# One core's mixture-of-experts tail: the last two experts' rows added on chip, the closing work dealt to three engines

## The chip, the cores and the metric

The kernel runs on one core of one Trainium2 chip. The metric is the time of one execution in device microseconds (us), the median of three runs. Beside it stands one execution recorded by the hardware profiler, from which every row below is taken. TensorE is called PE in the rows, VectorE DVE, ScalarE ACT, GpSimd POOL, SyncE SP.

## What is computed

One transformer layer for 256 prompt tokens and 64 sample tokens, 320 in all, with model width 1024, in float32. The change concerns only its last part: a mixture of 32 experts, of which each token takes two, and the closing layer norm.

```python
def hier_moe(h, p):                      # tok: 320 x 1024
    ...                                  # eid, w2: two experts of one group and their shares
    combine = jnp.einsum('nk,nke->ne', w2, jax.nn.one_hot(eid, N_EXPERTS, dtype=jnp.float32))
    y = jnp.zeros(tok.shape, jnp.float32)
    for e in range(N_EXPERTS):
        he = jax.nn.silu(tok @ p['w_exp_gate'][e]) * (tok @ p['w_exp_up'][e])
        y = y + combine[:, e:e + 1] * (he @ p['w_exp_down'][e]).astype(jnp.float32)
    ...
def trunk_layer(...):
    ...
    x = layer_norm(DEEPNORM_ALPHA * x + gate_f[:, None] * hier_moe(h, p), p['ln2_g'], p['ln2_b'])
```

## The kernel before

The program is written engine by engine, each engine's instructions in the order of the code; semaphores join them (`then_inc` counts up when an instruction is done, `wait_ge` holds an engine until a count is reached). After attention and routing, the kernel goes through the 32 experts one by one. Each expert has 64 slots, and each of its three weight matrices is 2 MB; SP loads them into a ring of nine buffers (`expert_chunk`), three experts deep, each load waiting until the buffer's former contents were used.

For one expert, in `step` on each engine: POOL gathers the token rows of the expert's slots from DRAM (`gather`, line 617), TensorE turns them (line 1448) and multiplies by gate and up matrices (`gate_up`, line 1458), ACT takes the silu (`silu`, line 959), DVE multiplies (`gated`, line 2022), TensorE turns the hidden rows (`turn_hidden`, line 1470), DVE copies them (`turned`, line 2026), TensorE multiplies by the down matrix (`down`, line 1481), and DVE scales the 64 result rows by the token's share and the condition's gate into a buffer `ystage` (`rows_out`, lines 2006 and 2012). POOL then scatters `ystage` into a DRAM table `expert_rows` (`scatter`, line 626). The table has four rows of 512 per token: two halves of width for each of its two experts. Which token sits in which slot is a one-hot table `onehot` (tokens by slots), written by DVE in `one_hots` and used by TensorE in `index` (line 1417). For tokens beyond an expert's 64 slots there is a loop over extra rounds (`n_over` of them), behind a branch on each engine; with these inputs it is not entered, as the trace has 32 scatters for 32 experts.

After expert 31 the end begins. POOL waits until every scatter has landed (`scattered0` to `scattered2`) and loads the table back, for the three token tiles in the order 0, 2, 1 (128, 64 and 128 tokens) into `comb[t]` (line 667), two rows of 1024 for a token side by side. `comb` lies in ring buffers 3 and 4, and the closing norm's vectors `ln2` in ring buffer 5, loaded by POOL once expert 29 is done with it (lines 647 and 648). TensorE adds in PSUM: for each tile a product of the identity with the scaled residual `x1` (line 1550), and products of the identity with each of the two rows in `comb[t]` (line 1556). DVE then handles the tiles one after another: statistics (lines 2116 and 2118), subtract the mean and multiply by the norm's weight (line 2122), the inverse deviation (lines 1579 to 1589, after ACT's square root at line 729), and multiply and add the bias (line 2125). ACT stores each tile (line 999), and the kernel ends when the last store has landed.

```python
            for t in LAST_ORDER:
                m = TR[t]
                pe.wait_ge(S[f"comb_in{t}"], 16)
                for c in range(2):
                    for k in range(2):
                        last = mm(fin_bank(t, c), ident[0:m, 0:m], comb[t][0:m, k * D + c * CB:k * D + c * CB + CB],
                                  start=False, stop=(k == 1))
                last.then_inc(S["fin_ps"], 1)
```

## Time and profile before

| | us |
|---|---|
| Median of three runs | 1040.59 (1039.27 to 1046.66) |
| Profiled execution, whole | 1043.44 |
| Profiled execution, span of the trace | 1041.7 |
| TensorE busy in the span | 945.7 |
| VectorE busy | 434.0 |
| ScalarE busy | 278.2 |
| GpSimd busy | 319.7 |
| Mean granted TensorE clock | 0.968 of full |

All times of rows are counted from the start of the span. From about 570 us to 990 us DMA moves 424 to 427 GB/s without a pause: this is the stream of expert weights. A row of a timeline merges consecutive instructions of one line; "x12" is their count. TensorE's float32 products are recorded as two instructions for each product. What stands in brackets at the end of a row is the idle time of the engine just before, and what ended it. Busy times on GpSimd are rough, as are the modelled ends of TensorE's products.

### The profile page before, as it was taken

How to read it: one execution, taken by the hardware profiler on the slowest of the kernel's cores; microseconds unless marked ns; L12 is line 12 of the kernel's file. 1: busy time of each engine (PE TensorE's matmuls, PEld its weight loads, DVE VectorE, ACT ScalarE, POOL GpSimd, SP SyncE). 2: the span in 40 equal slices, each digit the busy share in tenths (PEclk: the TensorE clock that was granted, in tenths of full speed). 3: DMA queues.
4: the chain of work that ended last, by engine and by line, in shares of the span. 5: the costliest groups of instructions: out<-in, count | busy, mean ns of one | idle time of the engine just before them, and what ended most of it. 6: DMA issues, size and time to landing. Idle time of an engine off the chain costs nothing.

```text
span 1041.7 us, 14676 instructions
## 1 busy us (share of the span) xinstructions
PE 945.7 (91%) x5901; PEld 627.7 (60%) x5913; DVE 434.0 (42%) x884; ACT 278.2 (27%) x466; POOL 319.7 (31%) x270
## 2 busy tenths in 40 slices
PE   4899998899997999999999999999998989898885
PEld 3689998896997988898753343444433333333321
DVE  4201078926451436768943332333332232232215
ACT  1453443251765567433341000000000000000100
POOL 7555477770432433560001111111111111111110
PEclk9999999999999999999979999999999999999997
DMA  9962445438577582387577999999999999999943
GB/s 327 330 126 62 87 108 127 73 92 238 154 168 229 159 278 84 131 295 286 223 316 298 425 424 425 425 425 427 425 424 426 427 424 427 425 426 425 425 177 119
DMA packets 61030, 294.08 MB, mean 282 GB/s; under 512 B 7473, under 2 KB 9113, under 8 KB 48114
## 3 DMA queue, kind: packets, MB, share of 16 engines
q1 hardware_dynamic: 49584, 272.68, 70.8%
q0 software_dynamic: 6480, 11.40, 3.3%
q10 hardware_dynamic: 4914, 9.28, 2.4%
q8 instruction: 37, 0.61, 0.2%
q14 instruction: 15, 0.12, 0.0%
HBM read 289.97 MB, written 14.68 MB: 292 GB/s over the span
## 4 chain that ended last, share of the span: by engine, by line
PE 53%; DMA 29%; DVE 8%; issue 4%; ACT 4%; POOL 1%; SPq 0%; POOLq 0%; ACTq 0%; DVEq 0%
DMA ring<-in_w_exp_up 18%; PE bank L1458 15%; DMA ring<-in_w_in 7%; PE bank L1481 6%; PE bank L1098 6%; PE bank L1100 6%; PE bank L1099 6%; DMA cond_slot<-in_w_cond 2%; PE bank L1049 1%; PE bank L1448 1%; DMA ring<-in_w_cond 1%; PE bank L1470 1%; DVE hf L2022 1%; DVE out_lo L1822 1%; ACT hf L959 1%
## 5 line engine op out<-in xcount | busy, mean ns | idle before, releaser
L567 POOL TENSOR_TENSOR w_lo<-ring,w_hi 128x1024 fp32r<-128x1024 f32 x76 | 183.7, 2429 | 168.3 <-ACT w_hi L772 168.3
L1458 PE MATMUL bank<-ring,hf 128*64 128x512 f32 x992 | 219.0, 593 | 14.1 <-DMA ring<-in_w_exp_up 14.0
L1098 PE MATMUL bank<-h_hi,w_hi 128*128 128x320 f32 x576 | 182.6, 317 | 9.0 <-POOL w_lo L567 8.0
L1100 PE MATMUL bank<-h_hi,w_lo 128*128 128x320 f32 x576 | 178.0, 309 | 0.0
L1458 PEld LDWEIGHTS bank<-ring,hf 128*64 128x64 f32 x992 | 75.4, 137 | 154.8 <-issue 144.2
L1481 PE MATMUL bank<-ring,he 128*64 128x512 f32 x512 | 132.6, 665 | 0.6 <-DVE he L2026 0.5
L959 ACT ACTIVATE hf<-bank 64x512 f32<-64x512 f32 x31 | 18.2, 588 | 425.8 <-PE bank L1458 425.8
L1099 PE MATMUL bank<-h_lo,w_hi 128*128 128x320 f32 x384 | 118.6, 309 | 0.0
L1098 PEld LDWEIGHTS bank<-h_hi,w_hi 128*128 128x128 f32 x576 | 108.1, 188 | 15.7 <-issue 10.1
L1100 PEld LDWEIGHTS bank<-h_hi,w_lo 128*128 128x128 f32 x576 | 108.1, 188 | 0.0
L617 POOL DMA_INDIRECT xrow<-expert_inputs,sidx x31 | 31.7, 1024 | 243.8 <-DVE sidx L2000 243.8
L2022 DVE TENSOR_TENSOR hf<-hf,bank 64x512 f32<-64x512 f32 x31 | 21.4, 690 | 196.4 <-ACT hf L959 196.4
L772 ACT ACTIVATE w_hi<-ring 128x1024 fp32r<-128x1024 f32 x76 | 79.7, 1051 | 31.3 <-DMA ring<-in_w_in 25.6
L626 POOL DMA_INDIRECT expert_rows<-ystage,sidx x32 | 32.6, 1017 | 179.1 <-DVE ystage L2012 179.1
L1481 PEld LDWEIGHTS bank<-ring,he 128*64 128x64 f32 x512 | 38.5, 153 | 72.2 <-issue 68.7
L1099 PEld LDWEIGHTS bank<-h_lo,w_hi 128*128 128x128 f32 x384 | 72.2, 188 | 0.0
L2012 DVE SCALAR_TENSOR_TENSOR ystage<-bank,share,hf 128x512 f32<-128x512 f32 x32 | 24.0, 750 | 90.5 <-issue 58.4
L1099 PE MATMUL bank<-oa_hi,w_hi 128*128 128x320 f32 x192 | 59.3, 309 | 0.0
L1676 DVE TENSOR_TENSOR pd<-pd,ka 128x640 f32<-128x640 f32 (+1 forms) x8 | 40.8, 5096 | 41.0 <-ACT pd L804 41.0
L1417 PEld LDWEIGHTS bank<-vcol,onehot 128*128 128x128 f32 (+1 forms) x192 | 26.1, 188 | 26.5 <-issue 25.2
L1470 PE MATMUL bank<-ident,hf 64*128 64x64 f32 x124 | 20.7, 287 | 21.3 <-DVE hf L2022 21.3
L1099 PEld LDWEIGHTS bank<-oa_hi,w_hi 128*128 128x128 f32 x192 | 36.1, 188 | 0.0
(405 smaller groups left out, 1317.9 us busy)
## 6 DMA issues: line engine op xcount, KB each, us to landing
ring<-in_w_exp_down SPq DMA_DIRECT2D x32, 2048.0 KB, 31.1
ring<-in_w_exp_gate SPq DMA_DIRECT2D x31, 2048.0 KB, 28.3
ring<-in_w_exp_up SPq DMA_DIRECT2D x31, 2048.0 KB, 32.6
ring<-in_w_in SPq DMA_DIRECT2D x15, 2048.0 KB, 13.8
cond_slot<-in_w_cond SPq DMA_DIRECT2D x9, 2048.0 KB, 11.7
ring<-in_w_cond SPq DMA_DIRECT2D x3, 2048.0 KB, 17.6
ring<-in_w_branch_b SPq DMA_DIRECT2D x2, 2048.0 KB, 8.4
ring<-in_w_branch_a SPq DMA_DIRECT2D x2, 2048.0 KB, 9.8
```

Of the source, the lines that this page charges most:

```text
L567: pool.tensor_tensor(w_lo_of[slot][:, :, c], raw[:, :, c], w_hi[:, :, c].bitcast(F32), ALU.subtract)\
L617: pool.indirect_dma_start(out=xrow[b][:, :], out_offset=None, in_=hbuf[:, :], in_offset=bass.IndirectOffsetOnAxis(ap=sidx[r][:, 1:2], axis=0),
L626: pool.indirect_dma_start(out=ybuf[:, :], out_offset=bass.IndirectOffsetOnAxis(ap=sidx[r][:, 0:1], axis=0), in_=ystage[b][:, :], in_offset ...
L772: X.activation(w_hi[:, :, c], raw[:, :, c], ACT.Copy).then_inc(S["hi_ready"], 1)
L1098: mm(b, hi[:, k, c], x_hi[:, k, :], start=(k == 0), stop=False)
L1099: mm(b, hi[:, k, c], x_lo[:, k, :], start=False, stop=False)
L1100: last = mm(b, lo[:, k, c], x_hi[:, k, :], start=False, stop=(k == KT - 1))
L1458: last = mm(bank[1][64 * q:64 * q + 64, :], xg[:, k % 4, k // 4, :], ring[s + q][:, k * FF:k * FF + FF], start=(k == 0), stop=(k == KT - 1 ...
L1470: last = nc.tensor.transpose(bank[6][:, f * SLOTS:(f + 1) * SLOTS], quarters[:, f, :], ident[0:SLOTS, 0:SLOTS])
L1481: last = mm(bank[3][64 * c:64 * c + 64, :], he[:, f, :], ring[s + 2][:, f * D + c * CB:f * D + c * CB + CB], start=(f == 0), stop=(f == FT ...
L1676: V.tensor_tensor(dl, dl, halves(ka, n)[0], ALU.mult)
L2022: V.tensor_tensor(gs[0:SLOTS, :], gs[SLOTS:P, :], bank[1][SLOTS:P, :], ALU.mult).then_inc(S["hrow_ready"], 1)
```

## The change

The rows of experts 30 and 31 no longer travel through DRAM. For these two experts TensorE turns the one-hot tables (three transposes in `index`), ACT copies them to SBUF (`slot_rows`, slots by tokens, in unused halves of `hf`), and at the end TensorE adds the experts' rows by products of these tables with `ystage` (`add_rows`): per token tile two products, each over 64 rows (one half of the width each). POOL scatters zeros in place of these rows, when their slots are known, so that the table in DRAM is complete after expert 29's scatter. SP loads `comb` behind the last weights, and then `ln2`.

TensorE then gets one base per tile in place of three inputs: DVE (tile 0, `rebase_first`) and POOL (tiles 2 and 1) add the two rows of `comb` and the residual `x1` beforehand. POOL first clears the lower half of tile 2's `comb`. The closing norm of tile 0 is done by ACT (subtract and scale, as a shift and a scale) and POOL (weight and bias, in two halves of the width); DVE keeps tiles 2 and 1. ACT stores in the order 2, 0, 1.

```diff
+        slot_rows = {E - 2: hf[:, 1, CB:CB + T], E - 1: hf[:, 0, CB:CB + T]}
+        zero_rows = gf_rows[:, 0, 0:CB]
+        shift = mv[:, 8:9, 0]
...
         @block.sync
...
             with sp.Else():
+                for b in range(3):
+                    sp.wait_ge(S[f"scattered{b}"], 16 * USES[b])
                 sp.nop()
+            sp.wait_ge(S["gu_ps"], E - 2)
+            for t in LAST_ORDER:
+                n = TR[t]
+                sp.dma_start(comb[t][0:n, :], ybuf[4 * P * t:4 * P * t + 4 * n, :].rearrange("(p k) d -> p (k d)", k=4))\
+                    .then_inc(S[f"comb_in{t}"], 16)
+            sp.wait_ge(S["down_ps"], E - 2)
+            sp.dma_start(ln2[:, 0, :], a["ln2_g"][0].partition_broadcast(P)).then_inc(S["ln2_in"], 16)
+            sp.dma_start(ln2[:, 1, :], a["ln2_b"][0].partition_broadcast(P)).then_inc(S["ln2_in"], 16)
...
         @block.gpsimd
...
             for n in range(1 + (E - 3) // 6 * 6, E - 2):
                 gather(n + 2, (n + 2) % 6, (n + 2) % 3, True)
+                if n + 2 in slot_rows:
+                    scatter_zeros(n + 2, (n + 2) % 6, (n + 2) % 3)
                 scatter(n, n % 6, n % 3)
-            scatter(E - 2, (E - 2) % 6, (E - 2) % 3)
...
-            scatter(E - 1, (E - 1) % 6, (E - 1) % 3)
...
+            pool.wait_ge(S["gu_ps"], E - 2)
+            ch.add(pool.memset(comb[2][SLOTS:P, 0:D], 0.0))
+            ch.done()
+            pool.wait_ge(S["x1_scaled"], 3)
+            for t in LAST_ORDER[1:]:
+                m = TR[t]
+                pool.wait_ge(S[f"comb_in{t}"], 16)
+                ch.add(pool.tensor_tensor(comb[t][0:m, 0:D], comb[t][0:m, 0:D], comb[t][0:m, D:2 * D], ALU.add))
+                ch.done()
+                pool.tensor_tensor(comb[t][0:m, 0:D], comb[t][0:m, 0:D], x1[0:m, t, :], ALU.add)\
+                    .then_inc(S["base_ready"], 1)
+            pool.wait_ge(S["ln2_in"], 32)
+            for c in range(2):
+                h = slice(c * CB, c * CB + CB)
+                pool.wait_ge(S["normed_first"], c + 1)
+                pool.tensor_tensor(x1[:, 0, h], x1[:, 0, h], ln2[:, 0, h], ALU.mult).then_inc(S["scaled_first"], 1)
+                pool.wait_ge(S["scaled_first"], c + 1)
+                pool.tensor_tensor(x1[:, 0, h], x1[:, 0, h], ln2[:, 1, h], ALU.add).then_inc(S["fin_ready0"], 1)
...
         @block.scalar
...
+                if e + 2 in slot_rows:
+                    act.wait_ge(S["slots_ps"], e + 5 - E)
+                    X.activation(slot_rows[e + 2], bank[7][:, 0:T], ACT.Copy).then_inc(S["slots_ready"], 1)
...
+                if i == 1:
+                    act.wait_ge(S["shift_ready"], 1)
+                    for c in range(2):
+                        X.activation(x1[:, 0, c * CB:c * CB + CB], fin_bank(0, c), ACT.Identity, bias=shift[:, 0:1],
+                                     scale=rstd[:, 0:1]).then_inc(S["normed_first"], 1)
...
         @block.tensor
...
+            def add_rows(e, t, start, stop):
+                pe.wait_ge(S["ys_ready"], e + 1)
+                pe.wait_ge(S["slots_ready"], e + 3 - E)
+                for c in range(2):
+                    half = slice(64 * c, 64 * c + 64)
+                    last = mm(fin_bank(t, c), slot_rows[e][half, TC[t]], ystage[e % 3][half, :], start=start, stop=stop,
+                              skip_group_check=True)
+                return last
+            add_rows(E - 2, 0, True, False)
             turn_hidden(E - 1)
             down(E - 1, base(E - 1), last_use)
...
-                        last = mm(fin_bank(t, c), ident[0:m, 0:m], comb[t][0:m, k * D + c * CB:k * D + c * CB + CB],
-                                  start=False, stop=(k == 1))
-                last.then_inc(S["fin_ps"], 1)
+                if t:
+                    add_rows(E - 2, t, True, False)
+                pe.wait_ge(*((S["base_ready"], LAST_ORDER.index(t)) if t else (S["base_ready0"], 1)))
+                for c in range(2):
+                    mm(fin_bank(t, c), ident[:, 0:m], comb[t][:, c * CB:c * CB + CB], start=False, stop=False,
+                       skip_group_check=True)
+                add_rows(E - 1, t, False, True).then_inc(S["fin_ps"], 1)
...
         @block.vector
...
+            def rebase_first():
+                dve.wait_ge(S["x1_scaled"], 1)
+                dve.wait_ge(S["comb_in0"], 16)
+                V.tensor_tensor(comb[0][:, 0:D], comb[0][:, 0:D], comb[0][:, D:2 * D], ALU.add).then_inc(S["base_part"], 1)
+                dve.wait_ge(S["base_part"], 1)
+                V.tensor_tensor(comb[0][:, 0:D], comb[0][:, 0:D], x1[:, 0, :], ALU.add).then_inc(S["base_ready0"], 1)
...
             with dve.Else():
+                rebase_first()
+                rows_out(E - 1, (E - 1) % 6, (E - 1) % 3, (E - 1) // 3)
                 dve.nop()
...
+            final_stats(0, 0)
+            final_stats(1, 2)
+            dve.wait_ge(S["nrm_sum"], 9)
+            reciprocal(9, 0, 1)
+            V.tensor_scalar(shift, mv[:, 0:1, 0], rstd[:, 0:1], -1.0, ALU.mult, ALU.mult).then_inc(S["shift_ready"], 1)
+            dve.wait_ge(S["ln2_in"], 32)
+            final_rows(1, 2)
+            final_stats(2, 1)
+            final_rows(2, 1)
```

`final_stats` and `final_rows` hold what the loop over tiles held before: statistics, and the rest.

The order of DVE's instructions from the turned hidden rows of expert 31 on, before (the two rows at lines 2006 and 2012 are `rows_out`; between them and the statistics stands the branch over the loop of extra rounds):

```order
L2022 TENSOR_TENSOR hf<-hf,bank 64x512 [waits gs_ready]
L2026 COPY he<-bank 128x256 [waits he_t]
L2006 SCALAR_TENSOR_TENSOR hf<-gf_rows,share 128x512 [waits sidx_ready]
L2012 SCALAR_TENSOR_TENSOR ystage<-bank,share,hf 128x512 [waits scattered1,down_ps,gate_chosen]
L2091 TENSOR_LOAD plan_i
L2091 ISA x2
L2092 COMPARE_AND_BRANCH
```

In the changed kernel the branch comes first, and on the side that is taken two additions on `comb[0]` stand ahead of `rows_out`:

```order
L2149 TENSOR_TENSOR ring<-ring 128x1024 [waits comb_in0,x1_scaled]
L2151 TENSOR_TENSOR ring<-ring,x 128x1024 [waits base_part]
L2062 SCALAR_TENSOR_TENSOR hf<-gf_rows,share 128x512 [waits sidx_ready]
L2068 SCALAR_TENSOR_TENSOR ystage<-bank,share,hf 128x512 [waits scattered1,down_ps,gate_chosen]
L2170 UNCONDITIONAL_BRANCH
L2180 BN_STATS stats<-bank 128x6 [waits fin_ps]
```

So the rows of expert 31 are now written behind two additions of 1024 columns each. The last instructions of POOL's queue in the changed kernel (`ring` is `comb` and `ln2`, `x` is `x1`), which before ended with the loads of `comb`:

```order
L690 MEMSET ring 64x1024 [waits gu_ps]
L696 TENSOR_TENSOR ring<-ring 64x1024 [waits comb_in2,x1_scaled,pool_chain]
L698 TENSOR_TENSOR ring<-ring,x 64x1024 [waits pool_chain]
L696 TENSOR_TENSOR ring<-ring 128x1024 [waits comb_in1]
L698 TENSOR_TENSOR ring<-ring,x 128x1024 [waits pool_chain]
L704 TENSOR_TENSOR x<-x,ring 128x512 [waits normed_first,ln2_in]
L706 TENSOR_TENSOR x<-x,ring 128x512 [waits scaled_first]
L704 TENSOR_TENSOR x<-x,ring 128x512 [waits normed_first]
L706 TENSOR_TENSOR x<-x,ring 128x512 [waits scaled_first]
```

These eight additions and products are new on POOL; the second and third have no wait on each other, and `comb_in1` is the only thing between them. TensorE's last instructions in the changed kernel, behind expert 31's down product:

```order
L1613 MATMUL bank<-ring,ident 128x512 [waits base_ready0]
L1613 MATMUL bank<-ring,ident 128x512
L1587 MATMUL bank<-ystage,hf 128x512 [waits slots_ready,ys_ready]
L1587 MATMUL bank<-ystage,hf 128x512
L1587 MATMUL bank<-ystage,hf 64x512 [waits slots_ready,ys_ready]
L1587 MATMUL bank<-ystage,hf 64x512
L1613 MATMUL bank<-ring,ident 64x512 [waits base_ready]
L1613 MATMUL bank<-ring,ident 64x512
L1587 MATMUL bank<-ystage,hf 64x512 [waits slots_ready,ys_ready]
L1587 MATMUL bank<-ystage,hf 64x512
```

Before, six products with `x1` and twelve with `comb` stood here; now tile 0 has four products, and tiles 2 and 1 six each, of which `ystage` rows mark those over 64 rows.

## Rows read from the trace of the kernel before

**Rows 1.** Chain of waits, from 900 us to the end (start, us, what)

```profile
940.02 38.22 DMA ring<-in_w_exp_up
...
993.64 7.10 PE bank L1458 x32
...
1007.10 0.76 DVE ystage L2012
...
1008.64 2.39 DMA expert_rows<-ystage,sidx
...
1011.76 5.80 DMA ring<-expert_rows
...
1017.60 6.31 PE bank L1556 x8
```

**Rows 2.** Timeline of the end, all engines (start, us, engine, line, operation)

```profile
1002.86 0.43 DVE L2026 COPY he<-bank 128x256 f32<-128x256 f32 x1 [0.78 <-PE bank L1470]
...
1003.34 3.65 PE L1481 MATMUL bank<-ring,he 128*64 128x512 f32 x16 [0.52 <-DVE he L2026]
...
1006.92 5.75 PE L1550 MATMUL bank<-x,ident 128*128 128x512 f32 x12
...
1024.01 1.30 DVE L2116 BATCH_NORM_STATS2 stats<-bank 128x6 f32<-128x512 f32 x2 [16.16 <-PE bank L1556]
...
1025.58 1.41 DVE L2122 SCALAR_TENSOR_TENSOR x<-bank,mv,ring 128x512 f32<-128x512 f32 x2
...
1027.66 1.28 DVE L2125 SCALAR_TENSOR_TENSOR x<-x,rstd,ring 128x1024 f32<-128x1024 f32 x1
...
1028.86 1.28 DVE L2116 BATCH_NORM_STATS2 stats<-bank 64x6 f32<-64x512 f32 x2
...
1038.63 0.34 ACTq L999 DMA_DIRECT2D out_y_prompt<-x  x1
```

**Rows 3.** Timeline of POOL, the scatter of expert 29

```profile
978.09 1.01 POOL L626 DMA_INDIRECT expert_rows<-ystage,sidx  x1 [4.46 <-DVE ystage L2012]
```

**Rows 4.** DMA issues by line (count, KB each, median us from issue to landing)

```profile
ring<-expert_rows POOLq DMA_DIRECT2D x2, 1024.0 KB, 7.4
...
expert_rows<-ystage,sidx POOLq DMA_INDIRECT x32, 7.9
```

**Rows 5.** Windows (us; busy of PE, PEld, DVE, ACT, POOL; granted clock; DMA share, GB/s)

```profile
1012.00:1016.00 4.00, 0.68 (x2) 0.00 (x0) 0.00 (x0) 0.00 (x0) 1.39 (x3) 1.00 0.69 252
1016.00:1023.00 7.00, 5.40 (x7) 2.30 (x8) 0.00 (x0) 0.00 (x0) 0.00 (x0) 0.51 0.77 232
...
994.00:996.00 2.00, 2.00 (x12) 0.86 (x10) 0.38 (x1) 0.00 (x0) 0.82 (x1) 1.00 0.62 262
996.00:1001.00 5.00, 4.72 (x23) 1.55 (x18) 0.00 (x0) 0.24 (x1) 1.34 (x3) 1.00 0.71 249
978.00:986.00 8.00, 7.09 (x32) 2.63 (x32) 0.00 (x0) 0.50 (x1) 1.01 (x1) 1.00 1.01 423
```

**Rows 6.** Timeline, VectorE and GpSimd between 129 and 148 us

```profile
129.97 5.43 POOL L567 TENSOR_TENSOR w_lo<-ring,w_hi 128x1024 fp32r<-128x1024 f32 x2 [1.45 <-ACT w_hi L772]
...
132.36 0.83 DVE L1676 TENSOR_TENSOR pd<-pd,ka 128x640 f32<-128x640 f32 x1 [0.62 <-ACT pd L804]
...
133.11 2.97 DVE L1677 TENSOR_TENSOR pd<-pd,qa 128x640 f32<-128x640 f32 x1
...
142.15 5.37 DVE L1676 TENSOR_TENSOR pd<-pd,ka 128x640 f32<-128x640 f32 x1 [3.08 <-ACT pd L804]
...
142.16 4.67 POOL L567 TENSOR_TENSOR w_lo<-ring,w_hi 128x1024 fp32r<-128x1024 f32 x2
```

**Rows 7.** Groups by shape, GpSimd (count, busy, mean ns, idle before)

```profile
L567 POOL TENSOR_TENSOR w_lo<-ring,w_hi 128x1024 fp32r<-128x1024 f32 x76 | 183.7, 2429 | 168.3 <-ACT w_hi L772 168.3
```

**Rows 8.** Timeline of TensorE, products over half of the rows

```profile
272.51 0.70 PE L1237 MATMUL bank<-qb,kb 64*128 64x256 f32 x4
...
273.05 0.39 PE L1239 MATMUL bank<-qb,kb 64*128 64x128 f32 x4
```

More of the change, by code:

```diff
@@ L391, in build, with fin_bank @@
         out_hi = (w_lo[1], w_hi)
+        def fin_bank(t, c):
+            return bank[((0, 4), (2, 6), (7, 5))[t][c]][0:TR[t], :]
         block = ctx.enter_context(nc.Block())
@@ L995, in _ @@
                 deviation(t, 1)
-            for i, t in enumerate(LAST_ORDER):
-                act.wait_ge(S["fin_ready"], i + 1)
+                if i == 1:
[3 more added lines that the diff above has]
+                                     scale=rstd[:, 0:1]).then_inc(S["normed_first"], 1)
+            for t in (2, 0, 1):
+                act.wait_ge(*((S["fin_ready"], LAST_ORDER.index(t)) if t else (S["fin_ready0"], 2)))
                 dst = out["y_prompt"][0][t * P:t * P + P, :] if t < 2 else out["y_sample"][0]
@@ L1414, in index @@
                     pe.wait_ge(S["sidx_ready"], n)
+                if isinstance(n, int) and n in slot_rows:
+                    if n == E - 1:
+                        pe.wait_ge(S["slots_ready"], 1)
+                    for t in range(3):
+                        m = TR[t]
+                        last = nc.tensor.transpose(bank[7][:, TC[t]], onehot[0:m, t, :], ident[0:m, 0:m])
+                    last.then_inc(S["slots_ps"], 1)
                 for t in range(3):
```

60 lines of the change are left out of this document (26 added, 34 removed).

## The prediction

> **What bounds the kernel now.** I read the chain of waits first, then the timeline of its last 60 us, then windows for DMA and clock. The chain shows where the stream of weights stops being the limit: 38.22 us of up-weights end at 978.2, and from there to the end the chain runs through engines alone [rows 1]. So whatever the change adds to TensorE before 978 lies under the DMA stream, and whatever it removes behind 978 counts in full, if nothing else becomes late. From expert 31's hidden rows on, the timeline reads: copy to 1003.29, down products 1003.34 to 1006.99, then TensorE does the six products with `x1` beside the rest [rows 2]. The rows of expert 31 are ready at 1007.86, their scatter has landed at 1011.03, the first load back at 1017.56, and only then do the products with `comb` start [rows 1]. The first tile's statistics begin at 1024.01; the last store is issued at 1038.63 [rows 2], 3.07 us before the span ends.
>
> So 16.15 us lie between the rows of expert 31 and the first statistics (1007.86 to 1024.01), and 17.7 us between these and the end. The change attacks the first stretch by taking scatter and load away, and the second by dealing out tile 0.
>
> **What goes.** The round trip: 2.39 us scatter, 0.73 us to POOL's next issue, 5.80 us load [rows 1]. Behind it, four products at the lower clock: TensorE sat idle from 1012.67 (1006.92 + 5.75, rows 2) to 1017.60, the granted clock in 1016 to 1023 was 0.51 (the 1.2 GHz level), and four products took 6.31 us [rows 1, 5]. At the full level six products took 5.75 [rows 2]. A pair of full products thus costs 1.92 us at 2.4 GHz, 3.16 at 1.2 GHz.
>
> **What comes, before the end.** The six transposes, two copies by ACT and two scatters of zeros lie before 978. The transposes are hidden by the DMA stream; without that cover they would cost at most 6 x 0.27 = 1.6 us (two products of 256 columns take 0.54 [rows 8], and a transpose has 128 columns). The zeros take part of the DMA stream itself: at most 2 x 0.26 MB at the 423 GB/s of that stretch [rows 5] = 1.2 us; nothing, if the few filled slots are all that is written. I take 0.4, so the down products of expert 31 end at 1007.4. The products of expert 30's rows for tile 0 stand between gate/up and the turning of expert 31, where TensorE waits for ACT and DVE; uncovered they cost 1.1.
>
> **When `comb` lands.** SP waits for expert 29's scatter, issued at 978.09 [rows 3], landing after 7.9 [rows 4]: 986.0. The loads then queue behind the last weights, on the same rings. DMA moves 423 GB/s until then and thins out in 994 to 996 (262) and 996 to 1001 (249, where `ln2` is part) [rows 5]; `ln2` is 1.05 of the 1.24 MB of the last window, so 0.2 MB of weights are left at 996, on the slowest rings; I put their end at 998.3, with 0.4 for the zeros in it. Behind it at 0.425 MB per us: tile 0 (1 MB) at 1000.9, tile 2 (0.5 MB) at 1002.1, tile 1 at 1004.6, `ln2` at 1007.1. The bounds for tile 2 are 999.5 (all rings even, 995.8 + 3.7) and 1004.5 (a load's 7.4 of rows 4 behind 997). So the loads are hidden, as the change says.
>
> **What the additions do to each other.** DVE's two additions for tile 0 have two SBUF operands of 1024 columns; the nearest row is 1.28 us [rows 2]. POOL's additions of 1024 columns cost 2.43 [rows 7]. The trace shows what happens when both run: at 133.11 DVE's product of 640 columns, 0.83 us when alone, takes 2.97 and ends 0.7 after POOL's instruction; at 142.15 it takes 5.37, through *two* POOL instructions in a row (142.16 to 146.83), and ends 0.69 later [rows 6]. So DVE's work with two SBUF operands stands still while POOL adds, and POOL keeps going if its next instruction has nothing to wait for. In the changed order that is so between POOL's second and third addition; between first and second, and third and fourth, POOL waits for itself and DVE gets in.
>
> Step by step: DVE is free at 1003.29 + 0.4, and the branch, now ahead of the additions, I set at 0.4 (between nothing, as TensorE's starts its next products at 1006.92 without a gap, and the 0.73 of POOL): 1004.1. POOL's first addition runs 1002.1 to 1004.55. DVE's first: to 1005.85. POOL's second and third: to 1010.7. DVE's second, the base of tile 0: to 1012.0. Then the gate (0.75) and the rows of expert 31 (0.76): 1013.5.
>
> TensorE is idle from 1007.4 to 1012.0, nearly as long as before, so I take the lower clock again: base 3.16, rows of expert 31 over 64 rows. For these the nearest row is two products of 256 columns over the two halves of the array: 0.54 us from start to next start [rows 8], so 1.08 for 512 (1.9 if they ran one after the other). At the mixed clock I take 1.9: tile 0 is complete at 1017.1. Tile 2: 1.08 + 1.92 + 1.08 = 4.1, complete at 1021.2. Tile 1 follows at 1025.3 (POOL's fourth addition ends at 1015.2, ahead of it), before DVE wants it at 1027.
>
> **The end.** From there DVE's chain decides: statistics 1.57 (1024.01 to 1025.58), inverse deviation of tile 0 and its shift 0.95, tile 2 3.36 (1025.58 to 1028.94), statistics 1.57, tile 1 3.36, store 3.07 [rows 2]: 13.9. POOL's four half-width instructions for tile 0 (1.25 each, half of rows 7) run at the same time, and tile 2's last product (two SBUF operands) is held behind two of them: 2.4, between 0 and 3.9. Sum: 1021.2 + 13.9 + 2.4 = 1037.5, against 1041.7: 4.2 us less. Off the profiled execution's 1043.44 that is 1039.2; its median is 2.85 lower, so **1036.4**. Of the 13.3 us to be had without contention (rival 1), nine go back to the additions' standstill and the clock.
>
> The trace shows the standstill (2.97 in place of 0.83), and at 142.15 one that went on past the end of POOL's instruction [rows 6]. The Trainium skill (SBUF — State Buffer, section "SBUF: two separate sides") has a rule for it: VectorE and GpSimd share a pair of ports under an exclusive lock, and whichever starts first holds it for the whole of its instruction. On the standstill the trace agrees; on the hand-over at the instruction's end it does not. By the letter of the rule the sum is that of rival 2, 1030.7, by the rows 1036.4.
>
> **The rivals.**
> 1. *No contention that matters* (POOL's additions fall beside DVE's, or the lock is short). Base at 1006.7, tile 0 complete at 1007.4 + 1.92 + 1.08 = 1010.4, tile 2 at 1014.5, end at 1028.4: 13.3 less, 1027.3. For it: no row shows such additions at this place, and DVE's products that read PSUM don't have two SBUF operands. Against: rows 6. Chance 0.18.
> 2. *The lock passes at each instruction's end.* DVE's second addition then runs 1008.3 to 1009.6, the rows are ready at 1011.1, no low clock: tile 0 at 1012.6 and, with 4.1, tile 2 at 1016.7, 13.9 and 1.2 of holding: 1031.8, or 1030.7. For it: at 132.36 DVE got in between two POOL instructions. Against: 142.15. Chance 0.15.
> 3. *Tile 2 lands behind 1004.1*, so DVE adds first: base 1009.2, tile 2 at 1016.3, end 1032.6: 1031.5. Chance 0.1.
> 4. *Slower.* POOL's four additions hold DVE throughout, since the gap at its own wait is too short: 1002.1 + 9.7 + 2.6 = 1014.4 for the base; after 7 us idle TensorE stays at 1.2 GHz through tiles 0 and 2: 3.16 + 2.1 + 8.2 gives 1027.9; 13.9 and a held 3.6 give 1045.4: 3.7 more, 1044.3. It decides as soon as tile 2 is complete later than 1025.4 (1041.7 - 13.9 - 2.4). Chance 0.08.
> 5. *The loads don't hide*: SP's waits or a slow ring bring tile 0 after 1009. Base 1011.6, end near 1037.4: the same time as forecast by another cause. Chance 0.07.
>
> The forecast has 0.42. Faster by over 1% (below 1030.2) needs rival 1, or half of 2 and 3: 0.3. Slower by over 1% (above 1051.0) lies beyond rival 4: 0.03. Within 1%: 0.67. About 1% is what a measurement of this kernel tells from no change. The range goes from rival 1 to just short of rival 4, 1027.0 to 1043.0.
>
> **What would show it.** In the profile of the changed kernel: `comb` of tile 2 landed near 1002; DVE's two additions (line 2149 and 2151) long, the second about 6 us where 1.28 is its price; the base of tile 0 at 1012; a granted clock of 0.5 behind it; tile 2 complete at 1021; DVE's product at the end of tile 2 about 3.7 long. Wrong, if both additions take 1.3 (rival 1), or if no DVE instruction overlaps two POOL additions (rival 2).

## The result and the profile after

The changed kernel takes 1031.99 us (median of seven runs, 1028.84 to 1035.2) against 1041.21 (1039.27 to 1046.76) for the kernel before, measured beside it: a ratio of 0.99 with a 95% interval of 0.9873 to 0.9927, 9.2 us less. The forecast was 4.2 less, and 1036.4. The profiled execution took 1029.5 us; its span is 1027.7.

The spans can't be set against each other as they stand. The stages ahead of the experts vary from one execution to the next: in the fourteen profiled executions of this study expert 1's gate/up products start between 555.89 and 564.09 us. From there to expert 31's it takes 432.55 us before and 433.1 to 433.8 in the thirteen others. So I measure everything from the first gate/up product of expert 31 to the end of the span and call that the stretch. Before, it runs from 993.64 [rows 1] to 1041.7: 48.06 us. After, from 989.26 to 1027.7: 38.44.

The chain of waits of the changed kernel near its end (start, us, what), to be set beside [rows 1]:

```profile
983.24 17.66 DMA ring<-expert_rows
...
1001.00 1.24 DVE ring L2149
...
1003.41 2.84 DVE hf L2062
...
1006.27 0.76 DVE ystage L2068
...
1007.08 2.13 PE bank L1587 x8
1009.22 1.86 PE bank L1613 x4
1011.08 1.03 PE bank L1587 x4
```

The scatter and the load behind the rows of expert 31 are gone from the chain. In their place stands a load that was issued early and is nevertheless late: the chain goes through it until VectorE's first addition. After that it passes through VectorE's gate, which takes 2.84 us here, and through TensorE.

The timeline of the same end (start, us, engine, line, operation; the first row is cut by the window that was asked for), for [rows 2]:

```profile
989.26 3.23 PE L1511 MATMUL bank<-ring,hf 128*64 128x512 f32 x14 [0.63 <-DMA ring<-in_w_exp_up]
...
998.48 0.42 DVE L2082 COPY he<-bank 128x256 f32<-128x256 f32 x1 [0.78 <-PE bank L1523]
...
998.96 3.65 PE L1534 MATMUL bank<-ring,he 128*64 128x512 f32 x16 [0.52 <-DVE he L2082]
...
1001.00 1.23 DVE L2149 TENSOR_TENSOR ring<-ring 128x1024 f32<-128x1024 f32 x1 [2.10 <-DMA ring<-expert_rows]
...
1002.26 1.22 DVE L2151 TENSOR_TENSOR ring<-ring,x 128x1024 f32<-128x1024 f32 x1
1003.24 2.45 POOL L696 TENSOR_TENSOR ring<-ring 64x1024 f32<-64x1024 f32 x1 [28.34 <-DMA ring<-expert_rows]
1003.41 2.83 DVE L2062 SCALAR_TENSOR_TENSOR hf<-gf_rows,share 128x512 f32<-128x512 f32 x1
...
1003.54 1.98 PE L1613 MATMUL bank<-ring,ident 128*128 128x512 f32 x4 [0.93 <-DVE ring L2151]
...
1005.77 2.68 POOL L698 TENSOR_TENSOR ring<-ring,x 64x1024 f32<-64x1024 f32 x1
1006.27 0.75 DVE L2068 SCALAR_TENSOR_TENSOR ystage<-bank,share,hf 128x512 f32<-128x512 f32 x1
...
1007.08 2.13 PE L1587 MATMUL bank<-ystage,hf 64*128 64x512 f32 x8 [1.55 <-DVE ystage L2068]
...
1008.26 1.30 DVE L2180 BATCH_NORM_STATS2 stats<-bank 128x6 f32<-128x512 f32 x2 [1.23 <-PE bank L1587]
...
1012.13 1.29 DVE L2180 BATCH_NORM_STATS2 stats<-bank 64x6 f32<-64x512 f32 x2 [2.33 <-PE bank L1587]
...
1016.78 2.37 DVE L2193 SCALAR_TENSOR_TENSOR x<-x,rstd,ring 64x1024 f32<-64x1024 f32 x1
1016.81 1.26 POOL L706 TENSOR_TENSOR x<-x,ring 128x512 f32<-128x512 f32 x1
1018.03 2.24 POOL L704 TENSOR_TENSOR x<-x,ring 128x512 f32<-128x512 f32 x1
...
1022.71 1.28 DVE L2193 SCALAR_TENSOR_TENSOR x<-x,rstd,ring 128x1024 f32<-128x1024 f32 x1
```

Read the starts. VectorE is through with the turned rows at 998.90 and waits 2.10 us for tile 0. Its two additions then run at their own price, 1.23 and 1.22, because GpSimd gets tile 2 only at 1003.24, after both have begun. GpSimd's first addition then holds the gate: 2.83 where 0.75 is usual. Rows of expert 31 to first statistics (1007.02 to 1008.26) is 1.2 us; it was 16.15. Against that, from gate/up to these rows it now takes 17.8 us (14.2 before), and from the first statistics to the end 19.4 (17.7 before). The sum is -14.9 + 3.5 + 1.8 = -9.6.

Windows of the changed kernel (busy of PE, PEld, DVE, ACT, POOL; granted clock; DMA share, GB/s), for [rows 5], and its DMA issues, for [rows 4]:

```profile
988.00:992.00 4.00, 3.37 (x18) 1.23 (x16) 0.75 (x1) 0.00 (x0) 0.00 (x0) 1.00 0.99 412
993.00:997.00 4.00, 4.00 (x20) 1.33 (x16) 0.00 (x0) 0.59 (x1) 0.00 (x0) 1.00 1.01 199
997.00:1002.00 5.00, 4.14 (x20) 1.62 (x20) 2.11 (x3) 1.58 (x2) 0.00 (x0) 1.00 0.98 225
1002.00:1004.00 2.00, 1.07 (x5) 0.30 (x2) 1.97 (x3) 0.00 (x0) 0.76 (x1) 1.00 0.83 315
1003.00:1014.00 11.00, 8.83 (x26) 2.62 (x27) 7.29 (x12) 0.59 (x2) 9.77 (x4) 1.00 0.14 55
```

```profile
ring<-expert_rows SPq DMA_DIRECT2D x2, 1024.0 KB, 19.4
...
expert_rows<-ystage,sidx POOLq DMA_INDIRECT x30, 8.0
```

Two things to see. The clock stays at 1.00 through the tiles' products; no 0.51 as before. And from 993 to 1002 the DMA engines are busy the whole time (share 0.98 to 1.01) but move only about 210 GB/s, half of the 412 just before. The loads run beside expert 31's work, as the change wants it, but for most of that time at half speed, and so VectorE still waits for the first of them.

### The profile page after: what moved, and what is told of

The parts are those of the page before. It is cut to its first block, busy times and chain, and to the rows that moved or that the text cites. A ratio compares the mean times of both kernels' runs of the same rounds, so it can differ in the third digit from the quotient of the medians.

```text
span 1027.7 us, 14725 instructions
## 1 busy us (share of the span) xinstructions
PE 936.0 (91%) x5919; PEld 624.7 (61%) x5919; DVE 437.8 (43%) x884; ACT 280.0 (27%) x470; POOL 334.7 (33%) x275
## 4 chain that ended last, share of the span: by engine, by line
PE 56%; DMA 26%; DVE 9%; ACT 3%; issue 3%; POOL 2%; SPq 0%; POOLq 0%; ACTq 0%; DVEq 0%
PE bank L1511 15%; DMA ring<-in_w_exp_up 15%; PE bank L1144 7%; PE bank L1534 7%; PE bank L1146 6%; PE bank L1145 6%; DMA ring<-in_w_in 4%; DMA cond_slot<-in_w_cond 4%; PE bank L1095 2%; DMA ring<-expert_rows 2%; PE bank L1501 1%; DMA ring<-in_w_cond 1%; PE bank L1523 1%; DVE hf L2078 1%; DVE out_lo L1878 1%
## 5 line engine op out<-in xcount | busy, mean ns | idle before, releaser
L1534 PE MATMUL bank<-ring,he 128*64 128x512 f32 x512 | 129.1, 650 | 0.6 <-DVE he L2082 0.5
L647 POOL DMA_INDIRECT expert_rows<-ystage,sidx x30 | 30.5, 1018 | 145.8 <-DVE ystage L2068 145.8
```

What stands on the lines that cost most here:

```text
L647: pool.indirect_dma_start(out=ybuf[:, :], out_offset=bass.IndirectOffsetOnAxis(ap=sidx[r][:, 0:1], axis=0), in_=ystage[b][:, :], in_offset ...
L1534: last = mm(bank[3][64 * c:64 * c + 64, :], he[:, f, :], ring[s + 2][:, f * D + c * CB:f * D + c * CB + CB], start=(f == 0), stop=(f == FT ...
```

## The experiments

Twelve runs, each with one edit on the changed kernel unless said otherwise. The table has their stretches; the text has what each told.

| kernel | stretch, us | ratio to before (95%) |
|---|---|---|
| before | 48.06 | |
| changed | 38.44; again 38.52 | 0.99 (0.9873 to 0.9927); 0.9917 (0.9888 to 0.9945) |
| x1 gate first | 37.35 | 0.9888 (0.9844 to 0.9932) |
| x2 additions on TensorE | 40.78 | 0.9902 (0.9867 to 0.9936) |
| x3 tile 0's norm on VectorE | 37.96 | 0.9865 (0.9829 to 0.99) |
| x4 late loads | 45.72 | 0.9969 (0.9942 to 0.9997) |
| x5 tiles 0, 1, 2 | 37.41 | 0.9875 (0.9827 to 0.9924) |
| x6 both engines start together | 42.74 | 0.9959 (0.9927 to 0.9991) |
| x7 tile 2 loaded last | 36.23 | 0.9897 (0.9856 to 0.9939) |
| x8 = x5 and x3 | 37.59 | 0.9889 (0.9854 to 0.9923) |
| x9 = x7 and x3 | 36.48 | 0.9891 (0.9856 to 0.9926) |
| x10 = x9, tile 2 on TensorE | 36.17 | 0.9878 (0.9843 to 0.9912) |
| x12 = x4, tile 1 in two loads | 45.82 | 0.998, a single execution of each, no interval |

**x6: close to the order that I had forecast.** VectorE waits for tile 2 as well, so that both engines start adding together. (In the prediction GpSimd starts 2 us ahead.)

```diff
                 dve.wait_ge(S["comb_in0"], 16)
+                dve.wait_ge(S["comb_in2"], 16)
```

> DVE waits for tile 2's load too before its two additions, so that it starts them together with GpSimd's; nothing else changes. This sets up the case that the prediction took as likeliest. Theory (DVE stands still while GpSimd adds, through two additions in a row where the second waits for nothing; GpSimd's second and third are such a pair): one of DVE's two additions takes over 5 us, the base of tile 0 is ready 8 to 10 us after the start of the pair, TensorE falls to the lower clock, and the end comes 6 to 9 us later than the 38.4 us of the changed kernel. Rival (the hand-over is at the end of each instruction): no addition of DVE takes over 3.8 us, and the end comes 3 to 5 us later.

The stretch is 42.74, 4.3 more than without the wait. The timeline of that place:

```profile
1011.16 1.22 DVE L2150 TENSOR_TENSOR ring<-ring 128x1024 f32<-128x1024 f32 x1 [4.36 <-DMA ring<-expert_rows]
1011.19 3.38 POOL L696 TENSOR_TENSOR ring<-ring 64x1024 f32<-64x1024 f32 x1 [28.62 <-DMA ring<-expert_rows]
1012.42 3.25 DVE L2152 TENSOR_TENSOR ring<-ring,x 128x1024 f32<-128x1024 f32 x1
1014.65 3.20 POOL L698 TENSOR_TENSOR ring<-ring,x 64x1024 f32<-64x1024 f32 x1
1015.58 2.83 DVE L2062 SCALAR_TENSOR_TENSOR hf<-gf_rows,share 128x512 f32<-128x512 f32 x1
...
1015.72 3.43 PE L1613 MATMUL bank<-ring,ident 128*128 128x512 f32 x4 [5.21 <-DVE ring L2152]
...
1017.82 2.79 POOL L696 TENSOR_TENSOR ring<-ring 128x1024 f32<-128x1024 f32 x1
```

The two engines take strict turns. VectorE's second addition is held by GpSimd's first alone and ends 1.1 after it (1014.57 to 1015.67); GpSimd's second stands still until then; the gate is held by GpSimd's second, ends at 1018.41, and GpSimd's third, which waits for nothing by program, stands still in its turn. No VectorE instruction of this stretch stays out through two of GpSimd's. So the step "POOL's second and third: to 1010.7" falls: between these two, which follow each other without a wait, VectorE gets in. By the ratio this order is worth 4.3 us off 1044.47. That is the size that I forecast, but it comes from a standstill of another shape, so the agreement is luck. The Trainium skill (SBUF — State Buffer, section "SBUF: two separate sides") gives the pair of ports to whichever instruction starts first, until that instruction ends; this stretch of the trace agrees.

The trace of before holds both behaviours, and I had read only one of them:

```profile
188.54 7.15 DVE L1676 TENSOR_TENSOR pd<-pd,ka 128x512 f32<-128x512 f32 x1 [1.13 <-ACT pd L804]
...
381.54 7.70 POOL L567 TENSOR_TENSOR w_lo<-ring,w_hi 128x1024 fp32r<-128x1024 f32 x3 [5.94 <-ACT w_hi L772]
...
384.27 2.73 DVE L1764 TENSOR_TENSOR sp_lo<-sp,sp_hi 128x512 fp32r<-128x512 f32 x1
```

The product of line 1676 at 142.15 [rows 6] stayed out through two GpSimd instructions, and at 188.54 through three whole ones. The subtraction at 384.27 ended at 387.00, in the middle of three GpSimd instructions that ran from 381.54 to 389.24 without a pause. Counted in the fourteen traces, only two lines of the program, 1676 and 1810 of before, stay out when a second GpSimd instruction follows the first at once, and they do so each time; every other VectorE instruction that was held there gets in. What sets these two lines apart is open.

**x1: is the gate's 2.83 us GpSimd's doing?** The gate of expert 31 is put ahead of VectorE's two additions.

```diff
...
+                V.scalar_tensor_tensor(out=gate_slot, in0=gate_step, scalar=share[r][:, 1:2], in1=gate_base, op0=ALU.mult,
+                                       op1=ALU.add).then_inc(S["gate_chosen"], 1)
                 rebase_first()
-                rows_out(E - 1, (E - 1) % 6, (E - 1) % 3, (E - 1) // 3)
...
+                V.scalar_tensor_tensor(out=ystage[b][:, :], in0=bank[3][:, :], scalar=share[r][:, 0:1], in1=gate_slot,
+                                       op0=ALU.mult, op1=ALU.mult).then_inc(S["ys_ready"], 1)
```

> The gate of expert 31 is computed ahead of DVE's two additions, while DVE waits for the first load; nothing else changes. All times are counted from the start of expert 31's gate and up products, where the changed kernel needs 38.4 us to the end. Theory (GpSimd's first addition holds DVE's gate): the gate takes 0.75 us in place of 2.83, the rows of expert 31 are ready about 2.7 us earlier, but the second tile waits for GpSimd's second addition and is complete only 0.9 us earlier: 37.5 us to the end. Rival (the 2.83 us are something else at this place, say the branch or a late share): the gate stays near 2.8 us wherever it stands, and the end does not move: 38.4 us.

```profile
1006.83 0.75 DVE L2173 SCALAR_TENSOR_TENSOR hf<-gf_rows,share 128x512 f32<-128x512 f32 x1
```

The gate takes 0.75 us, in VectorE's wait for tile 0, and nothing holds the rows of expert 31: they are ready 14.8 us into the stretch instead of 17.8. Of the 3.0 us gained there 1.1 reach the end (37.35), since TensorE is at tile 0's base until 16.1 and, behind the rows' products, waits 0.56 for GpSimd's base of tile 2.

**x3: does dealing out tile 0's norm help?** ScalarE's and GpSimd's part of it goes back to VectorE, which then norms tiles 0, 2 and 1 in turn.

```diff
...
             final_stats(0, 0)
+            dve.wait_ge(S["ln2_in"], 32)
+            final_rows(0, 0)
             final_stats(1, 2)
...
-            dve.wait_ge(S["ln2_in"], 32)
             final_rows(1, 2)
```

> Tile 0's closing norm goes back to DVE, in the order 0, 2, 1, and ScalarE and GpSimd no longer take part in it; early loads, tables and bases stay. Theory (the deal of the end gives little, since DVE waits for the second tile anyway and GpSimd's products hold DVE's last product of that tile): 38.0 us from the start of expert 31's products to the end, within 1 us of the 38.4 of the changed kernel, and no long product at the end of tile 2. Rival (the deal takes 3.4 us off DVE's chain): 41 us or more.

37.96, half a microsecond *less* than with three engines. VectorE now spends 6.2 us on tile 0, 1.2 of them a hold by GpSimd, where it had waited 2.33 for tile 2, and takes tile 2 up 2.3 us later. It makes up 2.1 of these at tile 2, since GpSimd's closing products no longer hold tile 2's last one (1.27 instead of 2.37) and tile 0's deviation and shift no longer stand in between. The rest of the difference lies behind the last store. GpSimd's queue ends with an instruction called drain (line 144). Below are its duration (ns) and its start in the changed kernel and in x3:

```profile
L144 POOLq DRAIN  x1: 7196/7196/7196, 1020.3 to 1020.3; - x1
...
L144 POOLq DRAIN  x1: 8272/8272/8272, 1010.9 to 1010.9; - x1
```

In both it ends 5.9 us after the end of GpSimd's last addition or product. In x3 that is long past; in the changed kernel it is 1027.51, 0.9 us after the last store has landed, and the span ends 0.2 us behind it. Up to the landing of the last store the changed kernel takes 37.39 us and x3 37.59. In the order 0, 1, 2 the same edit costs 0.5 (x5 to x8, 36.63 to 37.15) and 0.7 (x7 to x9, 35.40 to 36.11) up to that landing, and 0.2 up to the end of the span. So dealing tile 0's norm to three engines gains 0.2 to 0.7 us and gives 0.4 to 0.7 of it back to GpSimd's drain.

**x5: another order of tiles**, 0, 1, 2 in loads, products and norms.

```diff
-LAST_ORDER = (0, 2, 1)
+LAST_ORDER = (0, 1, 2)
...
```

> The order of the tiles is 0, 1, 2 in place of 0, 2, 1, for the loads, the additions, the products and the closing norm. Theory (the load of tile 2, which goes to 64 partitions alone, slows all loads that run beside it to half the rate): the first load lands 2 us earlier after the start of expert 31's products than the 11.7 us of the changed kernel, and packets of 8 KB take near 0.31 us until tile 2's come; the end about 1.5 us earlier, 37 us. Rival (reading the table of expert rows is slow whatever the order): the first load lands at 11.7 us again, and the end is within 0.7 us of 38.4.

```profile
1002.07 1.23 DVE L2149 TENSOR_TENSOR ring<-ring 128x1024 f32<-128x1024 f32 x1
```

37.41, 1.0 less. What shortens it is at the front: VectorE's addition starts at 1002.07 right behind the turned rows, 9.7 into the stretch and without a wait for DMA (11.7 with a wait of 2.10 in the changed kernel), and the gate takes 0.74, since GpSimd starts only at 1006.29. Tile 0's load landed 9.1 us into the stretch instead of 11.65, though it is the same load, first in the queue in both. That fits the theory that tile 2's load slows what runs beside it, and not the rival.

**x2: the additions themselves.** GpSimd's four additions are taken out, TensorE adds `x1` and the loaded halves of tiles 2 and 1.

```diff
-                ch.add(pool.tensor_tensor(comb[t][0:m, 0:D], comb[t][0:m, 0:D], comb[t][0:m, D:2 * D], ALU.add))
...
+                    for c in range(2):
+                        mm(fin_bank(t, c), ident[:, 0:m], x1[:, t, c * CB:c * CB + CB], start=False, stop=False,
+                           skip_group_check=True)
...
+                            mm(fin_bank(t, c), ident[:, 0:m], comb[t][:, k * D + c * CB:k * D + c * CB + CB],
+                               start=False, stop=False, skip_group_check=True)
```

> Asks what GpSimd's four additions are worth, beside their cost in held VectorE instructions. They are taken out; TensorE adds x1 and the two loaded halves of tiles 2 and 1 by identity products, as before the change (tile 0 stays with VectorE). Measured is the stretch from the first gate/up product of expert 31 to the end of the span, 38.4 us in the changed kernel. Theory: nothing holds VectorE's gate (0.75 instead of 2.83 us), so tile 0's statistics start some 0.7 us sooner; but TensorE pays three pairs of 1.98 us for each base instead of one, 4.0 us more for each of two tiles behind tile 0's, so tile 1 is late: a stretch of 41.5 us (40.5 to 42.5), +3. Rival: the holds cost as much as the additions give, TensorE has the idle time: 38.4 or less.

40.78, 2.3 more: tile 2's statistics start 25.1 us into the stretch instead of 22.9. So GpSimd's additions are worth their holds, by 2.3 us.

**x4: what is the hiding of the loads worth?** SyncE issues them only when the down products of expert 31 are done.

```diff
-            sp.wait_ge(S["gu_ps"], E - 2)
+            sp.wait_ge(S["down_ps"], E)
             for t in LAST_ORDER:
```

> Asks what it is worth that the combined rows load beside expert 31's work. SyncE waits until the down product of expert 31 is done before it issues the three loads; nothing else is changed. Theory: the loads are issued 13.2 us behind the first gate/up product of expert 31 and land 5 to 7.5 us later (tile 0), so tile 0's base, its products and all that follows are 7 to 9 us later than in the changed kernel: a stretch of 45 to 47.5 us instead of 38.4, and most of the change's gain is gone. The loads themselves then run without weights beside them. Rival: the end is bound by the additions and products behind the loads, which can wait: 41 us or less.

45.72: 7.3 of the 9.6 us that the change gains are gone. It also leaves the loads alone on the DMA engines, in the order 0, 2, 1, with the last factors behind them. The windows:

```profile
1006.00:1008.00 2.00, 0.00 (x0) 0.00 (x0) 0.00 (x0) 0.00 (x0) 0.00 (x0) 1.00 1.19 422
1008.00:1010.00 2.00, 0.00 (x0) 0.00 (x0) 1.59 (x2) 0.00 (x0) 0.00 (x0) 0.55 1.00 197
1010.00:1012.00 2.00, 1.09 (x2) 0.57 (x3) 1.97 (x3) 0.00 (x0) 0.87 (x1) 0.50 0.85 332
1011.00:1012.00 1.00, 1.00 (x2) 0.48 (x3) 0.96 (x2) 0.00 (x0) 0.87 (x1) 0.50 0.96 401
1011.00:1015.00 4.00, 4.00 (x6) 1.46 (x8) 1.27 (x2) 0.00 (x0) 3.79 (x2) 0.50 0.99 403
1013.00:1015.00 2.00, 2.00 (x4) 0.50 (x5) 0.00 (x0) 0.00 (x0) 1.92 (x2) 0.50 1.02 408
```

Full rate, half rate, full rate again, at a DMA share of 0.85 to 1.19. The half rate is tile 2's turn; 1011 to 1012 is tile 1 alone, and 1013 to 1015 are the two loads of the last factors alone. (The clock of 0.50 is the lower level that TensorE gets here after waiting 7.78 us; the base of tile 0 takes 3.78 us at it, 1.98 in the changed kernel.)

**x7: tile 2 last.** The order of x5, and the factors of the last norm are loaded ahead of tile 2.

```diff
             for t in LAST_ORDER:
                 n = TR[t]
+                if t == 2:
+                    sp.wait_ge(S["down_ps"], E - 2)
+                    sp.dma_start(ln2[:, 0, :], a["ln2_g"][0].partition_broadcast(P)).then_inc(S["ln2_in"], 16)
+                    sp.dma_start(ln2[:, 1, :], a["ln2_b"][0].partition_broadcast(P)).then_inc(S["ln2_in"], 16)
```

> Asks why the packets of 8 KB of the combined rows took about 600 ns in the changed kernel and only some 310 in most of before's loads. Order of the tiles 0, 1, 2, as in the run with that order, and the two loads of the last norm's factors are issued ahead of tile 2's load instead of behind all three. Theory: it is the load of tile 2, which writes 64 partitions, that runs at half the rate and slows the packets beside it; so with it at the very end the packets of tiles 0 and 1 take about 310 ns and those of the factors about 160, 70 or fewer of the 320 large packets take over 500 ns, and GpSimd's first addition (tile 1) starts 1.5 to 3 us sooner than in the run with the order 0, 1, 2, 11 to 12.5 us behind the first gate/up product of expert 31. The stretch: 36.5 us (35.5 to 37.5), against 37.4 there. Rival: the loads of the factors, or the queue as such, are what slows: the slow packets begin as early as there or earlier, and GpSimd starts no sooner.

```profile
996.00:1000.00 4.00, 4.00 (x22) 1.61 (x20) 0.00 (x0) 0.00 (x0) 0.00 (x0) 1.00 0.99 410
1000.00:1003.00 3.00, 2.92 (x14) 0.77 (x10) 0.48 (x1) 0.74 (x2) 0.00 (x0) 1.00 1.02 408
1003.00:1006.00 3.00, 2.22 (x12) 1.18 (x14) 2.15 (x4) 1.43 (x2) 0.00 (x0) 1.00 0.91 201
```

The windows show 410 GB/s until tile 2's turn at 1003 and 201 behind it. GpSimd starts 12.6 us into the stretch, 1.3 sooner than in x5 (a little less than the 1.5 expected), and the stretch is 36.23. Counted in the traces, of the 320 packets of 8 KB that bring the three tiles in:

```
kernel                   packets of 500 ns or more   median of these   median of the others
before                                 75                640                 311
changed (0, 2, 1)                     187                618                 316
x5 (0, 1, 2)                           91                622                 312
x7 (0, 1, factors, 2)                  43                627                 313
x12 (tile 1 in two halves)            180                646                 309
```

Tile 2 has 64 of these packets. In the changed kernel 187 are slow: with tile 2 in the middle of the queue and the DMA engines coming off the weights at different times (the tiles' first packet starts at 988.6, the weights' last at 993), packets of tiles 0 and 1 run beside those of tile 2 and are slow with them. That is inferred from the counts, since a packet's record doesn't name its tile. The factors' packets show it directly, being of 4 KB: in x7 they take 160 ns before 1003, and 314 to 324 between 1004 and 1006, in tile 2's turn. And the landing of tile 0, the first load in every queue, follows the place of tile 2: 11.65 us into the stretch in the changed kernel, 9.1 in x5, 8.0 in x7.

**x12: its 64 partitions, or its rows in memory?** As x4, with tile 1 loaded by two DMAs of 64 partitions.

```diff
+                step = 64 if t == 1 else n
+                for p in range(0, n, step):
+                    sp.dma_start(comb[t][p:p + step, :], ybuf[4 * (P * t + p):4 * (P * t + p + step), :]
+                                 .rearrange("(p k) d -> p (k d)", k=4)).then_inc(S[f"comb_in{t}"], 16)
```

> The run with the late loads again, where the loads stand alone: tile 0 (128 partitions) moved at 422 GB/s there, tile 2 (64 partitions) at 197, tile 1 (128 partitions) at 403. Now tile 1 is loaded by two DMAs, of partitions 0 to 63 and of 64 to 127, with the same rows and the same 8 KB for each. Theory: it is the 64 partitions that cost the rate; then tile 1 too moves at some 200 to 250 GB/s, and its 1 MB takes 4 to 5 us instead of 2.5. Rival: it is where tile 2's rows lie in memory, or that it is the smaller load; then tile 1 stays near 400. The stretch from the first gate/up product of expert 31 stays at 45 to 47 us either way, since GpSimd comes to tile 1 only some 8 us after its rows could be there.

```profile
1010.00:1012.00 2.00, 0.00 (x0) 0.00 (x0) 0.00 (x0) 0.00 (x0) 0.00 (x0) 1.00 1.00 422
...
1015.00:1018.00 3.00, 2.20 (x3) 1.17 (x4) 2.16 (x3) 0.00 (x0) 2.14 (x1) 0.50 1.00 210
```

Tile 1's megabyte, which moved at 401 GB/s in one piece (x4, 1011 to 1012), moves at 210 in two halves. The rows in memory are the same, so it isn't their place. Nor is it that each half is a smaller load: the factors' loads are of half a megabyte too, into 128 partitions, and moved at 408 (x4, 1013 to 1015). It is the 64 partitions. The Trainium skill says so (SBUF — State Buffer, section "Door 1: The DMA port swizzle (why `[64,N]` ≈ `[32,N]`)"): partitions 0 to 63 reach 8 of 16 ports, with a limit of about 218 GB/s. The traces agree (197 and 210, where such loads run alone).

**x8, x9, x10: a better version?** x8 joins x5 and x3, x9 joins x7 and x3, and x10 is x9 with tile 2 added by TensorE, so that GpSimd keeps two additions.

> Joins two edits that each gave about half a microsecond to one: the tiles in the order 0, 1, 2, and tile 0's closing norm on VectorE alone (no ACT, no GpSimd part). Theory: VectorE's chain bounds from tile 0's statistics on. They start 16.4 us behind the first gate/up product of expert 31 (as in the run with the order 0, 1, 2); VectorE then needs three times 4.9 us, waits some 0.6 us for tile 1 and loses about 1.2 us to GpSimd's additions; the last store takes 3 us more: a stretch of 35.7 us (35 to 36.8), against 38.4 in the changed kernel, 37.4 and 38.0 with one edit alone. Rival: what tile 0's norm on VectorE costs comes on top, since VectorE has less idle time in this order: 38 or more.

> Joins three edits: tile order 0, 1, 2; the factors' loads ahead of tile 2's load; tile 0's closing norm on VectorE alone. Measured as before from the first gate/up product of expert 31 to the end of the span (38.4 us in the changed kernel, 36.2 in the run with the first two edits, 37.6 in that with the first and the third). Theory: VectorE is the bound from tile 0's statistics on (16.4 us in, three tiles of 4.9, 3 to the end: 34.1 without any hold) and GpSimd's third and fourth addition, which now run 1.3 us sooner, still hold it for some 2 us: 36 us (35 to 37), no better than with two edits. Rival: the additions of GpSimd now end ahead of VectorE's long instructions, so nothing is held: 34.5 or less.

> As the run that joins three edits, and TensorE adds tile 2's x1 and loaded halves (three pairs of products instead of one), so that GpSimd is left with two additions, for tile 1, ahead of VectorE's long instructions. Theory: no instruction of VectorE is held behind tile 0's statistics, but tile 2 is complete some 28 us behind the first gate/up product of expert 31, 1.5 to 2 us after VectorE is free for it: a stretch of 35.9 us (35 to 37). If the holds are the whole difference, the tile-0 and tile-1 part of VectorE's chain takes 9.8 us from tile 0's statistics to the end of tile 1's last product. Rival: it is held all the same, or TensorE is later: over 37.

x8 came to 37.59, outside the 35 to 36.8 of its theory. Its start was as expected (16.4), but GpSimd's additions cost more than the 1.2 us put down for them:

```profile
1011.41 1.16 DVE L1633 SCALAR_TENSOR_TENSOR rstd<-newton,rstd 128x1 f32<-128x1 f32 x1
1012.61 3.45 DVE L2181 SCALAR_TENSOR_TENSOR x<-x,rstd,ring 128x1024 f32<-128x1024 f32 x1
1012.63 2.33 POOL L698 TENSOR_TENSOR ring<-ring,x 64x1024 f32<-64x1024 f32 x1
```

1.0 at a tiny instruction (0.16 alone) and 2.2 at the product (1.28 alone), which began in the records 0.02 us ahead of the addition and still lost to it. x9 (36.48) and x10 (36.17) came as expected. In x9 the tiny instruction is held again, for 2.1 us (2.28 instead of 0.16). In x10 nothing is held behind tile 0's statistics, tiles 0 and 1 take 9.85 us (9.8 expected), and tile 2 is then 1.67 late on TensorE. Both end near x7's 36.23, each with another last wait.

x10's median is 1031.79, and the changed kernel's on the same chip is 1035.17; their intervals overlap. By the stretch, x7 and x10 are 2.3 us better than the changed kernel, which the medians alone don't show.

**x11: the changed kernel again**, beside these.

> The changed kernel once more, unaltered, beside the two versions above on the same chip: a ratio of 0.985 to 0.995 to the kernel before, and 38.4 us (37.5 to 39.5) from the first gate/up product of expert 31 to the end of the span, if that stretch is as steady as the theory takes it to be. The rival, that the stretch itself varies by some us from one execution to the next, would show in a stretch outside these bounds.

0.9917, and a stretch of 38.52 against 38.44, while expert 1's start in the two executions differs by 6.9 us. So the stretch may be read to a few tenths, as far as one repetition tells; x4 and x12, which should not differ in it, are 0.1 apart.

## Why the prediction was right in sign and half in size

In the stretch's terms I forecast 43.9 us (1037.5 less 993.64); it is 38.4. The time lies inside my range, but not by the mechanism that I took as likeliest: of the signs that I named for it (tile 2 landed near 1002, a second addition of 6 us, the base at 1012, a clock of 0.5 behind it, a held product of 3.7) none came. By the steps:

1. **The round trip goes**: right. x4 puts 7.3 of the 9.6 us down to the loads' being early (1.8 of them are the clock of tile 0's base, 3.78 against 1.98).
2. **What lies before 978**: right in kind. From expert 1's gate/up to expert 31's it takes some 0.8 us more, where I took 0.4.
3. **When `comb` lands**: wrong, the step that failed first. I put tile 0 7.3 and tile 2 8.5 us into the stretch, at 0.425 MB per us for all three. They were used 11.7 and 14.0 in, with VectorE and GpSimd waiting for them. The rate of tile 2 is half of that, and it slowed what ran beside it. In x7, with tile 2 last, tile 0 landed 8.0 in: 3.6 of the 4.4 us by which I had it wrong are the place of tile 2. The trace of before could have told me, with its 75 slow packets. By the Trainium skill's page and section cited at x12, tile 2 alone would have been put 1.2 us later (0.5 MB at some 218 GB/s in place of 425, an estimate); what tile 2 does to the loads beside it, the larger part of the 5.5 us at tile 2, that sentence doesn't say.
4. **Who adds first**: wrong, as a consequence. With tile 2 behind VectorE's free time, VectorE's additions ran undisturbed (1.23 and 1.22, against the 1.28 taken), and the base was ready 14.2 us into the stretch instead of 18.4. That is rival 3. It gave tile 2 complete at 1016.3 and the end at 1032.6, or 22.7 and 39.0 into the stretch; measured 22.9 and 38.4. In time it gave 1031.5; the median is 1031.99. That it comes so near is in part luck: it has the base at 15.6, 1.3 us later than measured, and no hold of the gate, which cost 2.1. Its condition, which I gave a tenth, came from the half rate.
5. **GpSimd holds VectorE through a pair**: wrong (x6). I took it from the row at 142.15; the row at 384.27 of the same trace says the contrary, and the instructions of this end behave like that one. It did not decide, since the order of step 4 left only the gate to be held (2.1 us, x1).
6. **The lower clock**: not taken here. TensorE waited 0.93 and 1.55 us, not 4.6, and kept 1.00. In x6 and x4, after 5.21 and 7.78 us, the same base took 3.43 and 3.78, near the 3.16 of the forecast. So the price was right and the wait was not there.
7. **Rows of an expert over two halves**: 1.07 us for a pair at the full clock (2.13 for two pairs), against 1.08 from [rows 8]; the 1.9 taken was for a low clock that did not come.
8. **The end**: 13.9 and 2.4 for the held product. From tile 2's statistics to the end it took 15.57, so 1.7 came on top, and the term was 0.7 too large. Of the 1.7, 1.1 were held at the product (2.37 against 1.28) and 0.3 at the small instruction ahead of it; 0.6 are the end of the span behind GpSimd's drain, of which I had nothing; and the statistics and deviations took 0.3 less than I had put down.

Steps 3 to 7 together make tile 2 complete 22.9 us into the stretch instead of 27.6: 4.7 of the 5.4 us by which the forecast missed. Step 8 is the rest. What x3 adds is that the third part of the change, dealing tile 0's norm to three engines, earns nothing as it stands, since GpSimd's drain takes back what it gains. What is gained is gained by the early loads and by GpSimd's additions (2.3, x2). The rows' not passing through DRAM is what lets the loads be early; no run takes it away by itself, and x4, which keeps it and loads late, is still 2.3 us shorter than before.

## What to carry to other kernels

Before you put down a transfer at the bytes over the full rate, look at how many partitions it writes; a DMA share of 1.0 at half the GB/s is the sign, and such a load belongs behind the others, since it slows whatever runs beside it. Where two engines hold each other, it is the order of arrival that decides the price, so work out the landing times before the holding times. Look, too, at when an engine gets its last instruction: here GpSimd's drain ended 5.9 us behind its last product, and the kernel with it. And where an early part of a kernel varies by microseconds, measure from an event close ahead of the change; a stretch that repeats to 0.1 us (once, here) tells parts apart that medians don't.

## What the runs showed that was not expected

- A load of 64 partitions moves some 200 GB/s at a DMA share of 1.00, and packets of other loads in flight at that time take twice as long: 187 slow packets of 8 KB (618 ns instead of 316) where the load itself has 64, and packets of 4 KB at 314 to 324 ns instead of 160. Two loads of 64 partitions in a row don't add up to the full rate (210 GB/s).
- A VectorE instruction of a single column is held by GpSimd too: `rstd` took 2.28 instead of 0.16 in x9, 1.16 in x8, 0.45 in the changed kernel.
- In x8 VectorE's product and GpSimd's addition began within 0.02 us, and GpSimd won; in x6 they began within 0.03, and VectorE won. Which engine gets in is not read from the order of the recorded starts.
- GpSimd's drain at the end of the program ended 5.9 us after its last addition or product, in each of the thirteen traces with such an end. Where that product came late, the span ended 0.1 to 0.7 us later than it does behind the last store otherwise.
